# Moving a branch of gated products from the RWKV stage of a hybrid trunk kernel into its merge stage

## The reference

```
mod = silu(cond) @ w_ada + b_ada
gates = sigmoid(p[..., OFF_GATE:]).reshape(B, T, 3, 1024)
merged = (gates[..., 0, :] * (o_a @ w_po_a) + gates[..., 1, :] * (o_b @ w_po_b)
          + gates[..., 2, :] * (o_c @ w_po_c))
x = x + gt1 * (merged @ w_out)
x = x + gt2 * ((silu(gu[..., :D_FF]) * gu[..., D_FF:]) @ w_ffn_out)     # gu = h2 @ w_ffn_in
```

## Time and profile before

| | us |
|---|---|
| median of 3 runs | 2055.25 |
| lowest and highest run | 2050.95, 2056.38 |
| the profiled execution, its own time | 2054.59 |
| its span, first to last instruction | 2052.2 |
| TensorE busy | 1824.7 (89%) |
| VectorE busy | 1029.8 (50%) |
| ScalarE busy | 741.3 (36%) |
| GpSimd busy | 149.6 (7%) |
| mean granted TensorE clock | 0.949 of full speed |

### The profile page before, as it was taken

The page is one execution under the profiler, slowest core; times in us unless marked ns, Lnnn a source line. Parts: engine busy times, 40 slices in busy tenths (PEclk is TensorE's granted clock), DMA queues, the critical chain, the costliest instruction groups (busy, mean ns, idle before and its releaser), DMA issues.

```text
span 2052.2 us, 38879 instructions
## 1 busy us (share of the span) xinstructions
PE 1824.7 (89%) x16851; PEld 1554.5 (76%) x16851; DVE 1029.8 (50%) x1829; ACT 741.3 (36%) x1299; POOL 149.6 (7%) x325
## 2 busy tenths in 40 slices
PE   5899897868798799999989989888688879999998
PEld 3899455546475798999989975555566669899998
DVE  1436438887443455334342444597684355543332
ACT  2333444333232435333243443523342343433321
POOL 2000000034020000000000000000522000000000
PEclk8899999989898899999999999999898989999999
DMA  7443321202207443443443432311022233344432
GB/s 261 163 124 113 102 95 50 85 2 64 84 27 246 142 126 95 131 133 95 127 147 97 133 97 89 114 58 47 2 79 70 84 108 123 103 124 125 117 114 87
DMA packets 267936, 214.48 MB, mean 105 GB/s; under 512 B 7225, under 2 KB 259544, under 8 KB 267512
## 3 DMA queue, kind: packets, MB, share of 16 engines
q1 hardware_dynamic: 264816, 204.41, 32.7%
q0 software_dynamic: 2736, 7.54, 1.2%
q10 hardware_dynamic: 216, 0.06, 0.0%
HBM read 209.10 MB, written 2.88 MB: 103 GB/s over the span
## 4 chain that ended last, share of the span: by engine, by line
PE 58%; DVE 10%; ACT 3%; issue 3%; DMA 1%; ACTq 0%; POOL 0%; DVEq 0%; POOLq 0%
PE bank L559 10%; PE bank L564 10%; PE bank L560 10%; PE bank L618 4%; PE bank L1176 3%; PE bank L1174 3%; PE bank L1175 3%; PE bank L984 2%; PE bank L624 1%; DVE gate L2064 1%; PE bank L615 1%; PE bank L993 1%; PE bank L926 1%; PE bank L518 1%; DMA ring<-in_w_ada_dram 1%
## 5 line engine op out<-in xcount | busy, mean ns | idle before, releaser
L560 PE MATMUL bank<-scr_rounded 128*128 128x384 f32 (+1 forms) x1376 | 465.7, 338 | 0.0
L559 PE MATMUL bank<-scr_rounded 128*128 128x384 f32 x704 | 241.8, 343 | 39.2 <-ACT scr_rounded L1360 19.2
L560 PEld LDWEIGHTS bank<-scr_rounded 128*128 128x128 f32 (+1 forms) x1376 | 261.9, 190 | 1.0
L564 PE MATMUL bank<-scr_rounded 128*128 128x384 f32 x704 | 231.6, 341 | 0.0
L1804 DVE TENSOR_TENSOR scr_rounded<-ring,scr_rounded 128x2048 fp32r<-128x2048 f32 (+1 forms) x66 | 140.6, 2131 | 177.0 <-ACT scr_rounded L1349 176.2
L559 PE MATMUL bank<-scr_rounded,gate_rounded 128*128 128x384 f32 (+1 forms) x672 | 225.3, 335 | 2.6 <-DVE scr_rounded L1804 2.6
L564 PE MATMUL bank<-scr_rounded,gate_rounded 128*128 128x384 f32 (+1 forms) x672 | 225.2, 335 | 0.0
L1804 DVE TENSOR_TENSOR scr_rounded<-ring,gate_rounded 128x2048 fp32r<-128x2048 f32 (+3 forms) x66 | 134.7, 2041 | 121.8 <-ACT gate_rounded L1349 121.3
L618 PE MATMUL bank<-h,ring 128*128 128x384 f32 x512 | 192.3, 514 | 1.3 <-ACT mg L1341 1.3
L1349 ACT ACTIVATE scr_rounded<-ring 128x2048 fp32r<-128x2048 f32 (+1 forms) x66 | 117.9, 1786 | 150.8 <-PE bank L564 84.7
L559 PEld LDWEIGHTS bank<-scr_rounded 128*128 128x128 f32 x704 | 136.3, 194 | 43.0 <-issue 41.0
(11 more groups left out here) (379 smaller groups left out, 3184.2 us busy)
## 6 DMA issues: line engine op xcount, KB each, us to landing
ring<-in_w_in_dram SPq DMA_DIRECT2D x56, 1024.0 KB, 5.4
ring<-in_w_ada_dram SPq DMA_DIRECT2D x48, 1024.0 KB, 5.3
ring<-in_w_ffn_in_dram SPq DMA_DIRECT2D x88, 512.0 KB, 4.9
ring<-in_w_ffn_out_dram SPq DMA_DIRECT2D x32, 704.0 KB, 4.5
ring<-in_w_out_dram SPq DMA_DIRECT2D x8, 1024.0 KB, 4.9
ring<-in_w_po_a_dram SPq DMA_DIRECT2D x4, 1024.0 KB, 6.0
ring<-in_w_po_b_dram SPq DMA_DIRECT2D x4, 1024.0 KB, 6.4
ring<-in_w_po_c_dram SPq DMA_DIRECT2D x4, 1024.0 KB, 5.0
```

The source lines that it names most:

```text
L559: pe.matmul(o, w_hi[:, k, :], right[0][k], start=k == 0, stop=False)
L560: pe.matmul(o, w_lo[:, k, :], right[0][k], start=False, stop=False)
L564: ins = pe.matmul(o, w_hi[:, k, :], right[1][k], start=False, stop=k == nk - 1)
```

## The change

In each layer the two first gates of branch B stay plain in the GLA stage. Gates three and four (`gate_of(1, 2)`, `gate_of(1, 3)`) are done plain at once behind the RWKV barrier. The last four gates' weights (two chunks) and the whole projection of B (two chunks) are done in split form in the merge stage, ahead of the third branch; B's output is split for that (`src1_hi`, `src1_lo`), the gates get eight places of their own (`gates1`), and VectorE does the gating there. In the RWKV stage the plan has only the layer's last eight modulation blocks, at the eight places of the new `FILLS`. The next layer's eight modulation blocks go into the first layer's FFN: one after the norm's sum, then one after every second FFN chunk. The order of the weight transfers follows. The diff, with unchanged lines cut:

```diff
@@ -187,7 +187,9 @@
         squared = [h, arena[:, 23:31, :]]
-        last_gates = [pb[:, 4 + j, :] for j in range(4)] + [arena[:, 23 + j, :] for j in range(4)]
+        src1_hi, src1_lo = arena_r[:, 0:4, :], arena_r[:, 10:14, :]
+        gates1 = [gtmp[:, j, :] for j in range(2)] + [arena[:, 26 + j, :] for j in range(2, 8)]
+        last_gates = [pb[:, 4 + j, :] for j in range(4)] + [arena[:, 4 + j, :] for j in range(4)]
         ff_hi = [arena_r[:, NF + j, :] for j in range(12)] + [mg_r[:, j, :] for j in range(8)] + [take(T), gate_r[:, 7, :]]
@@ -336,7 +338,7 @@
 
-        PER.update(zeroed=0, strips_clear=0, squares=8, rstd=2, padded=2, ffo_half=8, normed=16, h_hi=24, h_lo=24, src_hi=1, src_lo=1, mg_hi=8, mg_lo=8, ff_hi=NF, ff_lo=NF,
+        PER.update(zeroed=0, strips_clear=0, squares=8, rstd=2, padded=2, ffo_half=8, normed=16, h_hi=24, h_lo=24, src_hi=2, src_lo=2, mg_hi=8, mg_lo=8, ff_hi=NF, ff_lo=NF,
                    att_squares=1, att_rstd=5, att_normed=5, att_keys=1, att_queries=1, att_max=24, att_probs=24,
@@ -354,8 +356,7 @@
 
-        FILLS = ((4, 4, 0, 2, 1, 1, 1, 0, 1, 1, 1, 2, 2, 2, 1, 1, 3, 2, 2, 2, 1, 3, 2, 2, 1, 1, 1, 2, 1, 1, 1, 2, 2, 2),
-                 (4, 4, 0, 2, 1, 1, 1, 0, 1, 1, 1, 2, 1, 1, 1, 1, 2, 2, 2, 1, 1, 2, 2, 2, 1, 1, 1, 2, 1, 1, 1, 2, 1, 1))
+        FILLS = (1, 0, 0, 1, 0, 0, 1, 0, 0, 0, 0, 1, 0, 1, 0, 0, 0, 1, 0, 1, 0, 0, 1, 0, 0, 0, 0, 0, 0, 0, 0, 0, 0, 0)
 
@@ -368,16 +369,11 @@
             if k == 4:
-                return []
-            later = [("ada", l + 1, j) for j in range(8)] if l + 1 < layers else []
-            plan = []
-            for j in range(8):
-                plan.append(po_of(1, j))
-                if j < 6:
-                    plan.append(gate_of(1, j + 2))
-                if j % 4 == 3:
-                    plan += ada[8 + j - 3:8 + j + 1]
-            return plan + later
+                return [gate_of(1, j) for j in range(2, 4)]
+            return ada[8:16]
+
+        def next_ada(l):
+            return [("ada", l + 1, j) for j in range(8)] if l + 1 < layers else []
 
@@ -393,14 +389,19 @@
                         order.append(chunk(work))
-            order += [(l, "gate", 8 + j) for j in range(4)] + [(l, "po", 4), (l, "po", 5)]
+            order += [(l, "gate", 6 + j) for j in range(2)] + [(l, "po", 2), (l, "po", 3)] + [(l, "gate", 8 + j) for j in range(4)] + [(l, "po", 4), (l, "po", 5)]
             order += [(l, "out", j) for j in range(4)]
-            order += [(l, "ffi", j) for j in range(NF)]
+            later = [chunk(work) for work in next_ada(l)]
+            order += later[0:1]
+            for j in range(NF):
+                order += [(l, "ffi", j)]
+                if j % 2 and later and j // 2 < 7:
+                    order += [later[j // 2 + 1]]
             order += [(l, "ffo", j) for j in range(16)]
...
         splits = [(l, name, j) for l, name, j in order
-                  if name in ("in", "gk", "inc", "out", "ffi", "ffo") or name == "gate" and j >= 8 or name == "po" and j >= 4]
+                  if name in ("in", "gk", "inc", "out", "ffi", "ffo") or name == "gate" and j >= 6 or name == "po" and j >= 2]
 
@@ -619,9 +620,8 @@
                     else:
-                        src = (pa[:, 0:4, :], pb[:, 4:8, :])[work[2]]
                         for k in range(4):
-                            ins = pe.matmul(b[:, 0:T], w[:, k, 128 * (j % 4):128 * (j % 4) + 128], src[:, k, :], start=k == 0, stop=k == 3)
+                            ins = pe.matmul(b[:, 0:T], w[:, k, 128 * (j % 4):128 * (j % 4) + 128], pa[:, k, :], start=k == 0, stop=k == 3)
                             if k == 1:
@@ -1072,7 +1072,7 @@
 
-                steps = iter(FILLS[l])
+                steps = iter(FILLS)
                 fill(next(steps))
@@ -1149,18 +1149,29 @@
 
+                side[0] = side_steps(side_plan(l, 4))
+                finish(l, 4)
+                for j in range(2, 4):
+                    proj(l, ("gate", 4 + j), [("A", ("gate1", l, 2 * j + i)) for i in range(2)], h_parts, ("h", l, 8) if j == 2 else None)
+                pe.wait_ge(S["src_lo"], told("src_lo", l, 1))
+                for j in range(2):
+                    proj(l, ("po", 2 + j), [("V", ("po1", l, 4 * j + i)) for i in range(4)], (tiles(src1_hi, 4), tiles(src1_lo, 4)))
                 for j in range(4):
-                    proj(l, ("gate", 8 + j), [("A", ("gate2", l, 2 * j + i)) for i in range(2)], h_parts, ("h", l, 8) if j == 0 else None)
-                pe.wait_ge(S["src_lo"], told("src_lo", l, 1))
+                    proj(l, ("gate", 8 + j), [("A", ("gate2", l, 2 * j + i)) for i in range(2)], h_parts)
+                pe.wait_ge(S["src_lo"], told("src_lo", l, 2))
                 for j in range(2):
...
                 norm_sum(l, 1)
+                side[0] = side_steps(next_ada(l)) if next_ada(l) else iter(())
+                fill(1)
 
...
                     proj(l, ("ffi", j), [("AV"[i], ("ffi", l, j, i)) for i in range(2)], h_parts, ("h", l, 16) if j == 0 else None)
+                    if j % 2:
+                        fill(1)
                 for j in range(8):
@@ -1328,15 +1339,7 @@
                     kind, l, br, j = t
-                    if br == 0:
-                        place = mg[:, j, :]
-                    elif br == 1:
-                        place = gtmp[:, j % 2, :]
-                        if j >= 2:
-                            act.wait_ge(S["branch_merged"], told("branch_merged", l, j - 1))
-                    else:
-                        place = last_gates[j]
-                        act.wait_ge(fill_ready, filled("po", l, 1, 7))
+                    place = mg[:, j, :] if br == 0 else gates1[j]
                     act.wait_ge(fill_ready, filled(*t))
@@ -1720,10 +1723,20 @@
                 first_split = splits.index((l, "gate", 10))
+                split(first_split - 6)
+                split_h(l, 1)
+                split(first_split - 5)
+                A(src1_hi, pb[:, 4:8, :], ACT.Copy).then_inc(*tells("src_hi"))
+                for j in range(4, 8):
+                    side_work("gate1", l, j)
+                    act.wait_ge(psum_ready, filled("gate1", l, j))
+                    b = bank("gate1", l, j)
+                    A(gates1[j], b[:, 0:T], ACT.Tanh, scale=0.5).then_inc(*empties("gate1", l, j))
+                    if j % 2:
+                        split(first_split - 6 + j // 2)
+                A(src_hi, pc[:, 0:4, :], ACT.Copy).then_inc(*tells("src_hi"))
                 split(first_split - 2)
-                split_h(l, 1)
                 split(first_split - 1)
-                A(src_hi, pc[:, 0:4, :], ACT.Copy).then_inc(*tells("src_hi"))
                 for j in range(8):
@@ -1790,12 +1803,7 @@
                     dve.wait_ge(*emptied("gate", *t[1:]))
-                    if t[2] == 0:
-                        stt(out=mg[:, j, :], in0=mg[:, j, :], scalar=1.0, in1=b[:, 0:T], op0=add, op1=mult).then_inc(*empties(*t))
-                    else:
-                        stt(out=gtmp[:, j % 2, :], in0=gtmp[:, j % 2, :], scalar=1.0, in1=b[:, 0:T], op0=add, op1=mult).then_inc(*empties(*t))
-                        dve.wait_ge(*last())
-                        tt(mg[:, j, :], mg[:, j, :], gtmp[:, j % 2, :], add).then_inc(*tells("branch_merged"))
+                    stt(out=mg[:, j, :], in0=mg[:, j, :], scalar=1.0, in1=b[:, 0:T], op0=add, op1=mult).then_inc(*empties(*t))
 
@@ -2320,12 +2328,27 @@
                 first_split = splits.index((l, "gate", 10))
-                split(first_split - 2)
+                split(first_split - 6)
                 for k in range(KD):
                     split_h(l, 1, k)
+                split(first_split - 5)
+                dve.wait_ge(S["src_hi"], told("src_hi", l, 1))
+                tt(src1_lo, pb[:, 4:8, :], value(src1_hi), sub).then_inc(*tells("src_lo"))
+                for j in range(2):
+                    split(first_split - 4 + j)
+                for j in range(8):
+                    side_work("po1", l, j)
+                    dve.wait_ge(psum_ready, filled("po1", l, j))
+                    b = bank("po1", l, j)
+                    dve.wait_ge(*(emptied("gate1", l, j) if j >= 4 else emptied("gate", l, 1, j)))
+                    stt(out=gates1[j], in0=gates1[j], scalar=1.0, in1=b[:, 0:T], op0=add, op1=mult).then_inc(*empties("po1", l, j))
+                    dve.wait_ge(*last())
+                    tt(mg[:, j, :], mg[:, j, :], gates1[j], add).then_inc(*tells("branch_merged"))
+                    if j == 3:
+                        dve.wait_ge(S["src_hi"], told("src_hi", l, 2))
+                        tt(src_lo, pc[:, 0:4, :], value(src_hi), sub).then_inc(*tells("src_lo"))
+                        split(first_split - 2)
                 split(first_split - 1)
-                dve.wait_ge(S["src_hi"], told("src_hi", l, 1))
-                tt(src_lo, pc[:, 0:4, :], value(src_hi), sub).then_inc(*tells("src_lo"))
```

## The result

The changed kernel takes 2063.16 us (median of 20 runs, 2054.50 to 2070.71) against 2055.23 us before (20 runs beside it, 2047.85 to 2063.75). The ratio is 1.004, 95% interval 1.0027 to 1.0054: 7.9 us slower. The forecast was 2048, faster, with a range of 2016 to 2068. The profiled execution took 2060.22 us with a span of 2058.1, against 2054.59 and 2052.2 before.

What follows compares the result with a forecast made beforehand. The prediction took TensorE to bound the kernel wherever it is dense, with gaps in the RWKV stages. RWKV -95.2, merge +77.8 and FFN +10.7 gave -6.7 us from the profiled 2054.59: 2048 us, range 2016 to 2068.

Steps and rivals of the forecast that it cites:

- the clock: RWKV stages: only the thinned places fall to the lower clock, which costs 3.5 us a layer.
- (d): RWKV head pair 1: Gram products come 9.4 us earlier, pair 2's merges follow 3.2 us closer; gain 12.6 us.
- rival 2: RWKV stages: the clock falls further and costs 14 us a layer instead of 3.5; 2069 us, chance 0.22.
- (a): RWKV opening: VectorE sets the pace and sheds one pair of side operations; gain 1.1 us.
- (e): RWKV head pairs 2 and 3: fills and a wait for modulation weights go; gain 20.4 us.
- the dense row: RWKV trace of 16 us with no filling and TensorE busy 13.3 us, where the granted clock was 1.00.
- (b): RWKV, in front of the next Gram products: a fill of 1.56 us goes; gain 1.5 us.
- (c): RWKV head pair 0: three fills between short TensorE steps go, VectorE's copies stand bare; gain 2.6 us.
- Merge: Merge stage: the gates and projection moved there add 38.9 us a layer, 77.8 us in all.
- FFN: First layer's FFN: of the next layer's eight modulation blocks one is free, seven take 1.53 us each; 10.7 us added.
- Transfers: Weight transfers: the same chunks are issued in another order; cost 0.
- Rival 1: RWKV stages: the fills come back whole, 51.3 us a layer instead of 34.7; 2015 us, chance 0.17.

Runs made afterwards that it cites:

- j3: The changed kernel plus unused products only where TensorE waits longest in the RWKV stages; 2058.30 us.
- a1: The changed kernel without the two plain gates behind the RWKV barrier in each layer, so part of the computation is missing; 2050.30 us.
- u1: The changed kernel with the next layer's eight modulation blocks back in the first RWKV stage, one at a time; 2058.16 us.
- e1: The kernel before with only the next layer's eight modulation blocks moved from the first RWKV stage to FFN; 2046.72 us.
- j1: The changed kernel plus 132 unused products in each RWKV stage, without transfers or side operations; 2083.80 us.
- j2: The changed kernel plus 396 unused products in each RWKV stage, without transfers or side operations; 2175.64 us.
- p1: e1 with the last two gates and their projections plain behind the RWKV barrier, modulation blocks reordered, fill pattern thinned evenly from pair 1 on; 2026.72 us.
- q1: p1 with the second layer's fill pattern of the kernel before in both layers; 2044.95 us.
- y: The changed kernel with the projection's first half and gates three and four kept in RWKV, nothing plain behind the barrier; 2051.29 us.

## Why the prediction was wrong

**The gain of the two RWKV stages was put too high, by 3.6 and 6.6 us. Two steps failed: the clock, the term of 3.5 us a layer, and in step (d) "the Gram products can follow VectorE's last term".**

**The clock.** "So dense RWKV work keeps the upper level by itself, and only the thinned places lose it": the grant fell to 0.79 and 0.81, where 0.83 to 0.9 was forecast. The work that stays took PE 139.6 us in the second layer before (199.7 less 36.5 for gates and 23.6 for the projection) and takes 149.2 now: 9.6 us more for the same instructions. With the two thirds that rival 2 counted on the chain this is 6.4 us a layer in place of 3.5, an estimate; j3 got 4.0 and 1.8 back by products in the waits alone. The steps (a) to (e) together gave 31.1 of their 38.2 us, so that 7.1 us are missing in this layer where the clock term had 3.5. The page "TensorE: Matmul & The Clock Gate" of the Trainium skill, section "HAM oscillation — how this bites in real kernels", says that bursts of matmuls between waits for a transfer start slow each time; the waits here are for VectorE. Pair 1 of after agrees (2.40 us for 1.69), the stretch of pair 2, at 0.97, does not. I had weighed that rule against the dense row and given it too little.

**(a)** gave -0.3 us for 1.1 (the first factors start at 1454.24, and at 1453.94 before): the opening runs at 0.59, and its products are themselves late. **(b) and (c)** gave 2.9 for 4.1. **(d)** gave 6.3 for 12.6. Of the missing 6.3, 3.0 are VectorE's last term, which came that much later in the pair and in a1, at the higher grant, did not. The other 3.2 are the Gram products behind it: (d) removed all modulation blocks from their way, but one of the eight that stay stands right in front of them, and VectorE still waits 2.35 us for its product (in a1 2.4 us of lag are left). **(e)** gave 22.3 for 20.4, already with the clock in it; in a1's execution the same stretches gave 17.0. All together 31.1 for 34.7 net in the second layer, 27.5 by a1's execution. In the first, 53.3 for 59.9: its work is equal to the second's, as forecast, but its stage is 3.0 us longer in this execution, at a grant of 0.79 for 0.81.

**Merge** was right: 37.0 for 38.9 in the second layer, the third branch 45.5 us behind the barrier for 46. **FFN**: 10.6 us by u1, 12.7 by e1, for 10.7. **Transfers** at 0 was right for the time and wrong for the reason: ScalarE does wait for FFN weights, up to 4.8 us, and PE is busy all the same.

So the sum went from -6.7 to +5.9 us in the profiled execution: 10.2 from the two RWKV stages (3.6 and 6.6), 2.1 from stretches the change doesn't touch, 0.3 from where the stages are divided and from the dense stages. The starts of the first RWKV stage lie between 404.9 and 410.8 us in the executions shown here, so that the 2.1 is scatter. Rival 1 (the fills come back whole) is out. Rival 2 had the right sign and mechanism, at 2069 a little too strong; its limit, a stage of 218.4 us beyond which the gain is gone, was met: 218.6 and 221.6.

**What the sum as a whole overlooked** is that the price of filling is not a constant. I walked out all of it at once and netted 31 us against 37. In j1 and j2 the first 27 us of PE time cost 0.45 each and the next 55 cost 0.8 each; so the last of the filling to go gives the least back, while the dense stages charge that work in full. The stage of after, with 28 us less in it than p1's, is only 7 us shorter (the patterns differ too). It also left out the portions: p1 and q1 do the same work and differ by 18.2 us. The forecast compared the end points and neither the margin nor the pattern.

## What to carry to other kernels

Filling between waits has a price that rises with how full the stage already is: here the same eight blocks cost 3.7, 11.3 or 21.5 us, and a microsecond of unused products cost 0.45 us at first and 0.8 later. Before moving all of it, price the last piece and the first piece apart, and move the dear ones only. Then spread what stays evenly: the portions alone were worth 18 us, more than the move of the tail itself, which with the old portions gained nothing clear. Look also at what still stands in front of the product that the next engine waits for. Work that needs no preparation belongs where TensorE would wait for preparation anyway, as behind a barrier.

## What the runs showed of the hardware

The granted clock is a result of one execution as much as of the kernel. The same 995 or so instructions took 42.28 us at 0.91 and 46.33 at 0.79; the pair before them took 52.35 at 0.72 and 49.96 at 0.88 in the same two executions. Over the 30 runs of the kernel before that stood beside e1, u1, a1 and y, the time falls by 9 us for each 0.01 of mean grant (correlation -0.77); for a1's twelve runs by 8 (-0.96). Which of the two follows the other, a correlation doesn't say, and between kernels the mean grant doesn't order the times: after and a1 have 0.940 and 0.939 and lie 13 us apart. And products whose result nobody reads, put where TensorE stands (j3), went with stages shorter by 2 to 4 us.
